# A hybrid mLSTM / forgetting-attention layer on eight cores: first stage re-ordered, w_up's copies issued in attention, and blocks 16 to 31 of x and the memory's keys transposed by DMA

## What is computed

```
h    = rmsnorm(x) ;  proj = h @ w_in                       # 8208 columns
A:   mLSTM memory, 4 heads, q/k of 128, v of 256, gates i and f per head and token
     C_t = f C_(t-1) + i v k^T ;  h_t = C_t q / max(|n q|, 1) ; rmsnorm per head, * sigmoid(o)
B:   forgetting attention, 8 heads of 128: softmax(q k / sqrt(128) + F_t - F_s) v, s <= t
x1   = x + rmsnorm((sigmoid(ga) * (h_a @ w_a) + sigmoid(gb) * (h_b @ w_b)) @ w_out)
u    = causal_conv3(rmsnorm(x1) @ w_up) ;  a, g = split(u)  # 2 x 2816 columns
out  = x1 + rmsnorm((gelu(g) * a) @ w_down)
```

## Time and profile before

| what | value |
|---|---|
| median of 3 runs | 1720.13 us (1717.43 to 1723.8) |
| the profiled execution's own time | 1722.58 us |
| span of its slowest core (core 2) | 1720.7 us |
| spans of cores 0 to 7 | 1705.0, 1709.4, 1720.7, 1704.4, 1717.9, 1711.5, 1717.8, 1710.4 |
| busy on core 2: PE, PE load, DVE, ACT, POOL | 95%, 54%, 48%, 53%, 25% |
| the chain that ended last, by engine | PE 83%, DVE 4%, ACT 4%, issue 4%, DMA 3% |

### The profile page before, as it was taken

One profiled execution on the slowest core, in us unless ns is written; L12 is line 12 of the kernel. 1 busy time (PEld: TensorE's weight loads), 2 busy tenths in 40 slices (PEclk: granted clock), 3 DMA queues, 4 the chain that ended last, 5 costly groups with the idle time before them and its releaser, 6 DMA issues.

```text
span 1720.7 us, 36342 instructions; the slowest of 8 cores (1704.4 to 1720.7 us)
## 1 busy us (share of the span) xinstructions
PE 1627.5 (95%) x12448; PEld 932.6 (54%) x12448; DVE 828.3 (48%) x1605; ACT 909.4 (53%) x1715; POOL 432.1 (25%) x557
## 2 busy tenths in 40 slices
PE   4789978899999999999998999999999999999998
PEld 2345535455776776776776555555455444444443
DVE  4564535455334334343343222232887387485782
ACT  3565635555576677677778422222665164362461
POOL 1010101101111111111112233232843343343442
PEclk9899989999999999999999999999999999999999
DMA  9361546423622121231222421214574253443421
GB/s 302 124 191 62 78 71 117 81 50 64 101 36 31 27 42 24 33 48 23 33 35 60 105 98 50 98 50 182 155 243 151 62 185 110 135 154 92 147 99 49
DMA packets 102226, 163.22 MB, mean 95 GB/s; under 512 B 72864, under 2 KB 75168, under 8 KB 92832
## 3 DMA queue, kind: packets, MB, share of 16 engines
q1 hardware_dynamic: 78576, 134.50, 25.2%
q0 software_dynamic: 23040, 25.69, 10.4%
q10 hardware_dynamic: 432, 0.72, 0.1%
HBM read 160.63 MB, written 30.15 MB: 111 GB/s over the span
## 4 chain that ended last, share of the span: by engine, by line
PE 83%; DVE 4%; ACT 4%; issue 4%; DMA 3%; POOL 1%; DVEq 0%; ACTq 0%; SPq 0%; POOLq 0%
PE psum L381 51%; PE psum L1100 10%; PE psum L1652 9%; PE psum L1244 6%; PE psum L1575 5%; DVE arena L528 2%; ACT arena L1224 2%; DMA ha_scr<-arena 2%; ACT arena L536 1%; PE psum L513 1%; PE psum L826 1%; DMA arena<-norm_mix_pre 1%; DVE arena L494 1%; POOL arena L351 0%; DMA arena<-wup_scr 0%
## 5 line engine op out<-in xcount | busy, mean ns | idle before, releaser
L381 PE MATMUL psum<-arena 128*128 128x512 bf16 (+3 forms) x6796 | 1128.8, 313 | 42.1 <-ACT arena L536 12.2
L381 PEld LDWEIGHTS psum<-arena 128*128 128x128 bf16 x6796 | 566.0, 99 | 465.2 <-issue 70.8
L1224 ACT ACTIVATE arena<-psum,arena 128x512 bf16<-128x512 f32 (+1 forms) x576 | 371.2, 651 | 143.8 <-PE psum L381 132.3
L1608 DVE SCALAR_TENSOR_TENSOR arena<-psum,arena 128x511 f32<-128x511 f32 x352 | 254.9, 747 | 47.2 <-POOL arena L1597 18.2
L1100 PE MATMUL psum<-arena 128*128 128x512 bf16 (+3 forms) x896 | 219.2, 348 | 3.7 <-DVE arena L1077 2.6
L1077 DVE CAST arena<-psum 128x512 bf16<-128x512 f32 (+3 forms) x164 | 104.2, 642 | 245.6 <-PE psum L1100 133.3
L1244 PE MATMUL psum<-arena 128*128 128x129 bf16 x2112 | 214.1, 220 | 1.4 <-POOL arena L1229 1.2
L1244 PEld LDWEIGHTS psum<-arena 128*128 128x128 bf16 x2112 | 155.4, 98 | 70.1 <-issue 2.6
L1652 PE MATMUL psum<-arena 128*128 128x512 bf16 x704 | 153.1, 379 | 0.3
L1591 ACT ACTIVATE arena<-psum,arena 128x512 f32<-128x512 f32 x176 | 135.5, 778 | 22.2 <-PE psum L381 20.1
L1229 POOL TENSOR_TENSOR arena<-arena 128x128 bf16<-128x128 bf16 x128 | 59.1, 469 | 336.7 <-ACT arena L1224 335.2
(11 more groups left out here) (117 smaller groups left out, 1212.2 us busy)
## 6 DMA issues: line engine op xcount, KB each, us to landing
arena<-wup_scr SPq DMA_DIRECT2D x44, 1024.0 KB, 5.2
arena<-x SPq DMA_DIRECT2D x33, 512.0 KB, 5.0
arena<-w_merge SPq DMA_DIRECT2D x32, 512.0 KB, 5.0
arena<-w_mem SPq DMA_DIRECT2D x12, 1024.0 KB, 9.0
wup_scr<-w_up POOLq DMA_DIRECT2D x11, 1024.0 KB, 10.3
arena<-x SPq DMA_DIRECT2D x8, 1024.0 KB, 7.4
out<-arena SPq DMA_DIRECT2D x15, 512.0 KB, 2.9
arena<-w_fox POOLq DMA_DIRECT2D x24, 256.0 KB, 4.5
```

The lines of the kernel that those rows point to most:

```text
L381: ins = e.matmul(out_ap, lhsT=l, rhs=r, start=(i == 0), stop=(i == n - 1))
L1224: pg.add("act", lambda e: e.activation(out=pt.ap[:, c0:512], in_=bank(lgb)[:, 0:512 - c0], func=AF.Exp, scale=float(P) ** -0.5, bias=bias_ ...
L1608: pg.add("dve", lambda e, ups=ups, yb=yb, cidx=cidx, sh=sh, jw=jw, ag=ag, w_=w_: e.scalar_tensor_tensor(out=yb.ap[:, ag, sh:w_], in0=ups[: ...
```

## The change

In the memory stage: cst0 and norm_mix_pre are loaded in the other order; in the stage of blocks 0 to 7 squares and scaling run one block further ahead of the transpose; the first two projections of V stand between the steps of the gates; the second transpose of a two-tail iteration gets a PSUM bank of its own; and steps of the gates stand later. Blocks 16 to 31 are no longer transposed by TensorE: `A_sc` puts down a DMA transpose right behind the scaling, on semaphore trA0 or trA1 by the block's parity. The keys of own chunks are transposed by four DMAs of 128x128 each. The copies of w_up leave the memory stage, and attention issues them at each n % 48 == 44. Cut to what the text below speaks of:

```diff
+        aload(wpre_bc, wpre_bc.ap, vec["norm_mix_pre"].partition_broadcast(P), ALL, "c_wpre")
         aload(cst0, cst0.ap, cst0_d[:, :], ALL, "c_cst0")
-        aload(wpre_bc, wpre_bc.ap, vec["norm_mix_pre"].partition_broadcast(P), ALL, "c_wpre")
...
                 reads=[xg, (rstd.u, b), wpre_bc], writes=[xsb])
+            if b >= DMA_T0:
+                xb_, xd_ = xnT(b * P, P)
+                dma_T(xd_, xsb.ap, [xsb], [(xb_.u, b)], "trA%d" % (b % 2))
             if b - 4 in LOAD_AT:
...
-        def A_T(b):
+        DMA_T0 = 16
+
+        def A_T(b, tb_=None):
+            if b >= DMA_T0:
+                return
             xsb = xs[b % 2]
             buf, dst = xnT(b * P, P)
-            tb_ = (TB, RB[0])[b % 2] if b < 8 else TB
+            if tb_ is None:
+                tb_ = (TB, RB[0])[b % 2] if b < 8 else TB
...
+        def gates_slot3(s_):
...
             def k_trans(c):
-                lc = lcol(c)
-                pb = bank(TB).bitcast(BF16)
...
+                lc, k_ = lcol(c), ksb(c)
+                for h in range(4):
+                    dma_T(k_.ap[:, h, :], qkT.ap[:, 1, h, lc:lc + P], [(qkT.u, (1, h))], [(k_.u, h)], "trK%d" % (MPOS[c] % 2))
...
             A_G(0)
+            A_sc(2)
+            A_sq(3)
+            A_rstd()
             for b in range(2, 8):
-                A_sc(b)
+                if b < 6:
+                    A_sq(b + 2)
                 if b < 7:
-                    A_sq(b + 1)
+                    A_sc(b + 1)
                 A_T(b)
+                A_rstd()
                 if b < 7:
                     K_proj(b - 1)
                 A_G(b - 1)
...
             gates_slot(0)
-            W_cast(3)
+            vb0 = V_mm(0, 0)
             gates_slot_b()
+            vb1 = V_mm(1, 0)
             gates_slot_c()
...
                 for b in tails[1:]:
-                    A_T(b)
+                    A_T(b, SB1)
                     A_sc(b + 1)
                     A_sq(b + 2)
+                if late is not None:
+                    gates_slot3(late)
...
-                if 15 <= ip < 15 + NG:
-                    conv_job(ip - 15)
...
+                    if n % 48 == 44 and n // 48 < NG:
+                        conv_job(n // 48)
```

More of the change, by code:

```diff
@@ L567, in gates_slot2 @@
             pg.add("dve", lambda e: e.tensor_copy(out=totM.ap[:, sl, :], in_=tps[:, :, 0:4]), reads=[uT], writes=[(totM.u, s_)])
+        def gates_slot3(s_):
+            sl = slice(8 * s_, 8 * s_ + 8)
+            lps, tps, uL, uT = loctot.ap[:, 0, :, :], loctot.ap[:, 1, :, :], loctot, loctot
             acti(locF.ap[:, sl, :], lps[:, :, 4:12], AF.Copy, [uL], [(locF.u, s_)])
@@ L688, in V_proj, with V_mm @@
             def V_proj(c, hv):
+                V_ev(c, hv, V_mm(c, hv))
+            def V_mm(c, hv):
                 buf, xv = xnT(c * P, P)
@@ L692, in V_proj, with V_ev @@
                          bank_u[bk], [(buf.u, c)] + Wd_(2 + hv))
+                return bk
+            def V_ev(c, hv, bk):
                 v_ = vw[MPOS[c] % 2]
@@ L711, in QK_proj @@
                                  bank_u[bk], Wd_(qk) + [(tb.u, c + j) for j in range(nb_)])
+                        if nb_ == 1 and h % 2 == 0:
+                            sts(qkT.ap[:, qk, h, 0:w_], bank(bk)[:, 0:w_], (P ** -0.5) if qk == 0 else 1.0,
+                                [bank_u[bk]], [(qkT.u, (qk, h))])
+                            continue
                         acti(qkT.ap[:, qk, h, 0:w_], bank(bk)[:, 0:w_], AF.Copy, [bank_u[bk]], [(qkT.u, (qk, h))],
@@ L906, in build_program @@
                     W_cast(2)
+            W_cast(3)
             A_G(7)
             gates_slot(0)
-            W_cast(3)
+            vb0 = V_mm(0, 0)
             gates_slot_b()
+            vb1 = V_mm(1, 0)
             gates_slot_c()
@@ L916, in build_program @@
             gates_slot2(0, SB1)
-            V_proj(0, 0)
-            V_proj(1, 0)
+            V_ev(0, 0, vb0)
+            V_ev(1, 0, vb1)
+            gates_slot3(0)
             A_sq(8)
             A_sc(8)
+            V_proj(0, 1)
             A_sq(9)
-            V_proj(0, 1)
             aload(cst1, cst1.ap, cst1_d[:, :], ALL, "c_cst1")
@@ L959, in build_program @@
                     num_mm(c)
-                    if late is not None:
+                    if late is not None and not fresh:
                         gates_slot_c()
@@ L985, in build_program @@
                         QK_proj(cn)
+                    if own(c) and fresh and late is not None:
+                        gates_slot_c()
                     I_mm(cn)
@@ L998, in build_program @@
                     num_fin(c, 1)
-                if gs is not None:
+                if gs is not None and not own(c):
                     gates_slot(gs)
@@ L1004, in build_program @@
                     V_proj(cn, 1)
+                if gs is not None and own(c):
+                    gates_slot(gs)
                 if own(c) and cn is not None:
```

## The result

The changed kernel takes **1767.53 us** (median of 4 runs, 1763.28 to 1784.35) against 1719.05 (1717.43 to 1723.8) of the kernel before: ratio **1.0296 [1.0225, 1.0366]**. It is slower. The forecast was 1752 us with a range of 1724 to 1782, so the time lies inside the range and 15.5 us above the forecast: +48 us where I had +32.

A forecast was written before the change was run, and what follows sets the result against it. TensorE was taken as the bound, about 1705 us on a core without the ha_scr stall. Waits 48, clock 21 and copies 1, less gains of 25, made +45 us on such a core; forecast 1752 us, range 1724 to 1782.

The forecast's parts named there:

- +4.7, +3.2: Waits for later blocks' DMA transposes: QK_proj(16) ends 4.7 us later, and O_proj in iteration 14 costs 3.2 us.
- The wait: Iterations 15 to 19: O_proj waits on a shared semaphore for a block ten further on; +6.4 us each, 32 us.
- Rival 1: The wait isn't there or its DMA is in time; 1685 us, faster; chance 0.10.
- The clock: Behind each of nine idle stretches TensorE runs 4.8 us at half clock, losing 2.4 us: 21 us.
- rival 2: The wait bites but the clock stays and gains are at their upper end; 1725 us; chance 0.10.
- The first stage and the bank: Memory stage: re-ordered first stage gains 11 us; own bank for the second transpose in iterations 1, 3, 4 gains 6.6.
- Iteration 8: With iteration 9: A_G waits for DMA transposes of blocks 20 and 21, taken at 3.4 us to landing; +7.9 us.
- rival 3: DMA transposes land late, at 5.5 us, behind other DMAs; 1771 us, or 1782 with small gains; chance 0.12.
- Attention: Four of eleven w_up copies precede a causal mask on GpSimd's queue; +1 us, bounds 0 to 2.3.
- The keys' transposes: Four DMAs per iteration on SP's queue, 0.33 to 1.25 us each, wanted an iteration later; cost 0.
- transposes off TensorE: Memory stage: 5 blocks at 0.44 us and 11 keys at 0.22 us leave TensorE, a gain of 4.6 us.
- 11 + 6.6 + 3: Memory-stage gains: first stage 11 us, bank for the second transpose 6.6, moved steps of the gates 3.

The follow-up runs named there:

- own_sems: The changed kernel with one semaphore for each of blocks 16 to 31 in place of two for all: 1710.17 us, ratio 0.9943.
- mod4: The changed kernel with four semaphores for x's DMA transposes, by b % 4, in place of two: 1722.53 us, ratio 1.001.
- mod5: The changed kernel with five semaphores for x's DMA transposes, by b % 5, in place of two: 1750.13 us, ratio 1.0187.
- conv_alone: The kernel before with only w_up's copies moved to attention, at n % 48 == 44: 1724.84 us, ratio 1.0019.
- pe_quarters: The changed kernel with x's blocks and the keys all transposed by TensorE, and w_up's copies as quarters in attention: 1700.06 us, ratio 0.9888.
- copies_in_mem: The changed kernel with a semaphore per x block and w_up's copies left in the memory stage: total not used, memory stage 445.7 us.
- x_on_pe: The changed kernel with all 32 blocks of x transposed by TensorE, only the keys by DMA: 1704.01 us, ratio 0.9897.

## Why the prediction was right

The sum, on core 1, step by step against the starts of upd and num_mm of the kernel before:

| stretch | predicted | measured |
|---|---|---|
| up to iteration 8 (first stage, bank) | -17.6 | -12.5 |
| iterations 8 to 10 | +7.9 and 2 x 2.4 = +12.7 | +16.2 |
| to num_mm of iteration 15 | +4.7, +3.2 and 2 x 2.4 = +12.7 | +10.8 |
| iterations 15 to 19 | 5 x (6.4 + 2.4) = +44 | +42.7 |
| the rest of the stage | -7.6 | -4.8 |
| memory stage | +44 | +52.4 |

- **The wait** was right in place, cause and size. The periods of iterations 15, 16, 17 and 19, 19.4, 17.8, 17.5 and 17.8 us, stand against 18.4 (iteration 18, with its QK_proj, grew from 24.3 to 33.1), and own_sems, mod4 and mod5 show that the count does it. Rival 1 fell: the DMA took 3.06 us to land, as the earlier trace rows promised, and it was issued too late.
- **The clock** was right within its error. The x24 group would take 5.53 - 1.74 = 3.8 us at full clock (the earlier trace rows less a projection); the six behind waits took 5.41 to 6.50, 5.9 on the mean: 2.1 us each where I had 2.4. It fell every time, which rival 2 denied.
- **The first stage and the bank** were priced too high, 17.6 us where 12.5 came. The instruction that stood at 60.70 on core 2, the second half of the first upd, on core 1 before and after:

```profile
60.69 0.27 PE L826 MATMUL psum<-arena 128*128 128x256 bf16 x1 [2.11 <-ACT arena L536]
52.20 0.27 PE L839 MATMUL psum<-arena 128*128 128x256 bf16 x1 [0.84 <-ACT arena L544]
```
That is 8.5 us of the 11. The other 4.0 by iteration 8 stand against 6.6 for the bank: its waits of 2.3 to 2.4 us in iterations 1, 3 and 4 are gone, but TensorE is idle for 1.6 to 1.8 us at each of 63.9, 77.5 and 91.7, the first two for VectorE's root and scaling.
- **Iteration 8** was too cheap, with iteration 9 by 3.5 us: I took 3.4 us to landing where it was 9.34, because a weight load and a load of x stood just ahead on the queue. That was rival 3's mechanism, in one place only.
- **Attention** was wrong in kind, though its +1 was near. I took +1 for the copies' issue on GpSimd; the issue costs nothing, the bytes do. In this execution it was +1.5 us on the mean, in conv_alone +4.4, on single cores up to 14; that the changed kernel's +1.5 is so close to my +1 is luck. My bounds of 0 to 2.3 hold this execution's mean and neither conv_alone's nor single cores, since I asked only which queue the copies stand on.
- **The keys' transposes** were taken at 0 on the ground that they are put down early. They are issued 2.28 us apart, above my upper end of 1.25. In the changed kernel other waits covered it; with own semaphores it shows, as 7.3 us at three upd and a stage 4 us longer than with the keys on TensorE. The 4.6 us that I gave for transposes off TensorE are there iteration by iteration (8.74 us for 8.97 in the last ones, in the changed kernel too), and no kernel keeps them: with own semaphores the waits for the DMAs take them back.
- **The total**: core 1's span grew by 51.9 us, 7 above the sum, and the slowest core's span 1761.3 against 1753. So 8 of the 15.5 us between 1752 and 1767.53 stand in the profiled execution; the others come from its having been the fastest of four, where I had put the median 2.4 us below it. The gain of 16 us on the slow cores came as said: the longest landing of a write to ha_scr on core 2 is 4.6 us now. The eight cores differ by 9.7 us where I had 6.

Without the over-long waits the change is worth 10 to 20 us. The re-ordering of the memory stage (first stage, bank and gates) accounts for that: the stage is 386.8 us in pe_quarters and 404.1 in conv_alone, which differ in it and the pieces of the copies only, 17.3 us (I had 11 + 6.6 + 3).

The Trainium skill has a rule for this case (DMA: Bandwidth & Descriptors, "Why a DMA increments its semaphore by 16 and not by 1"): "One semaphore per in-flight slot, not one per stream." It gives it for the sake of data that has not landed. The kernel here avoids that by waiting for the full count, and the runs show what this costs in time: 57 us between two semaphores and sixteen.

The Trainium skill's advice to use TensorE where PSUM will do (VectorE: DVE Perf Modes, Rules for kernel authors), which I had set aside as changing nothing, is borne out by the totals here: the memory stage is 386 to 387 us with TensorE's transposes for x, for the keys or for both, and 391 with neither. It was not tried against keys' DMAs that need not wait for one another.

## What to carry to other kernels

Before a DMA is put in place of an engine's work, list who waits on its semaphore and for what count: with cumulative counts every reader waits for the youngest DMA put down on that semaphore, needed or not, and the spacing of reader and writer decides how often (five semaphores were worse than four). Read the issue times of like DMAs in a row: if they are as far apart as one takes to land, they wait for one another. And a large copy is not free because nothing waits for it; compare the stage that it leaves and the one that it enters on every core, not on the slowest alone.

## What the runs showed of the hardware that I had not expected

- A DMA transpose of 128x128 bf16 from SBUF to SBUF takes 1.08 us of SP's queue at the least and 2.2 us to land, one of 128x1024 takes 1.24 and 3.06: eight times the bytes for 0.16 and 0.9 us more. Four keys cost SP nearly four blocks.
- A transpose issued 0.4 us behind 1.5 MB of loads held the queue for 3.50 us and landed after 9.34; ahead of the same loads it took 1.22 and 3.56. Beside copies of w_up, in copies_in_mem, one landed after 18.3, and a plain load of x after 19.8.
- TensorE loses time beside DMA traffic that it does not wait for: up to 9.4 us in idle times over 1 us on a core beside eleven copies (x_on_pe), nothing on the eight cores of copies_in_mem and 4 us on two of eight in the kernel before, without them there; and not the same on two cores of one execution. How is not shown.
